# The same steps of a two-block layer stack on one core, merged in another order

## The reference, cut to what matters

```python
# block one, per layer: one wide projection, sparse attention beside a gated delta rule
proj = rms_norm(x, norm_gain[layer]) @ w_in[layer]                 # 1024 x 9304
y_a = dsa_attention(q_a, k_a, v_a, q_i, k_i, w_i) * silu(z_a)      # 64 keys of each query's indexer
o_b = chunked_gated_delta_rule(q_b, k_b, v_b, beta, g)             # needs a triangular inverse per chunk
x = x + (gate0 * y_a + gate1 * rms_norm(o_b) * silu(z_b)) @ w_out[layer]
...
x = rms_norm(x, final_gain)
# block two, per layer: projection, four attention branches, gated merge, output, layer norm
h = x @ w_in                                                       # 1024 x 3620
...
merged = merged + merge_g[:, :, n] * (yb @ w_branch[n])            # n = 0..3
out = merged @ w_out
x = layer_norm(ALPHA * x + out, ln_g, ln_b)
```

## Time and profile before

| | us |
|---|---|
| median of 3 runs | 1119.81 |
| lowest and highest | 1117.81, 1120.29 |
| the profiled execution, its own time | 1118.74 |
| its span in the trace | 1116.9 |
| PE busy | 1056.6 (95%) |
| POOL, DVE, ACT busy | 662.7, 624.0, 595.4 |

### The profile page before, as it was taken

One profiled execution on the slowest core, in us unless ns is written; L12 is line 12 of the kernel. 1 busy time (PEld: TensorE's weight loads), 2 busy tenths in 40 slices (PEclk: granted clock), 3 DMA queues, 4 the chain that ended last, 5 costly groups with the idle time before them and its releaser, 6 DMA issues.

```text
span 1116.9 us, 16760 instructions
## 1 busy us (share of the span) xinstructions
PE 1056.6 (95%) x6282; PEld 914.2 (82%) x6282; DVE 624.0 (56%) x1195; ACT 595.4 (53%) x998; POOL 662.7 (59%) x286
## 2 busy tenths in 40 slices
PE   5999999999979999999999998899999889999986
PEld 5988898888867897899888887788888668888865
DVE  3765349674555449526875555508455660645664
ACT  4654348654633574435665555345586534548651
POOL 3775446753626877445666445687545876754483
PEclk9999999999989999999999999899999999999999
DMA  8554235542333655342554333665333555533251
GB/s 293 167 173 130 82 113 151 151 133 76 113 132 111 186 170 151 97 131 82 152 145 132 95 114 106 179 187 153 100 103 96 191 162 170 151 118 105 87 190 53
DMA packets 80575, 151.59 MB, mean 136 GB/s; under 512 B 6448, under 2 KB 12400, under 8 KB 80496
## 3 DMA queue, kind: packets, MB, share of 16 engines
q1 hardware_dynamic: 80496, 150.54, 44.8%
HBM read 149.47 MB, written 1.05 MB: 135 GB/s over the span
## 4 chain that ended last, share of the span: by engine, by line
PE 85%; DVE 7%; ACT 3%; issue 2%; POOL 1%; DMA 1%; DVEq 0%; SPq 0%; ACTq 0%; POOLq 0%
PE bulk L905 49%; PE bulk L893 12%; PE chain L995 9%; PE chain L926 6%; PE bulk L898 1%; PE chain L1260 1%; PE chain L1241 1%; POOL w_lo L842 1%; PE chain L1115 1%; PE chain L1131 1%; DVE arena L1708 1%; ACT arena L1300 1%; PE chain L986 1%; DVE arena L1786 1%; DVE arena L1783 1%
## 5 line engine op out<-in xcount | busy, mean ns | idle before, releaser
L842 POOL TENSOR_TENSOR w_lo<-raw,w_hi 128x1024 fp32r<-128x1024 f32 (+4 forms) x277 | 648.8, 2357 | 431.7 <-ACT w_hi L1300 431.4
L1300 ACT ACTIVATE w_hi<-raw 128x1024 fp32r<-128x1024 f32 (+4 forms) x277 | 279.7, 1019 | 202.0 <-PE bulk L905 164.2
L905 PE MATMUL bulk<-w_hi,hT_hi 128*128 128x512 f32 (+1 forms) x756 | 308.5, 408 | 12.8 <-DVE arena L1786 6.6
L905 PE MATMUL bulk<-w_hi,hT_lo 128*128 128x512 f32 (+1 forms) x756 | 296.3, 392 | 0.0
L905 PE MATMUL bulk<-w_lo,hT_hi 128*128 128x512 f32 (+1 forms) x756 | 296.0, 392 | 0.0
L905 PEld LDWEIGHTS bulk<-w_hi,hT_hi 128*128 128x128 f32 x756 | 143.7, 190 | 47.9 <-DVE arena L1786 8.8
L905 PEld LDWEIGHTS bulk<-w_hi,hT_lo 128*128 128x128 f32 x756 | 143.4, 190 | 30.5
L905 PEld LDWEIGHTS bulk<-w_lo,hT_hi 128*128 128x128 f32 x756 | 143.9, 190 | 26.6 <-issue 1.0
L1300 ACT ACTIVATE arena<-chain 128x512 f32<-128x512 f32 (+4 forms) x92 | 62.0, 685 | 120.1 <-PE chain L926 106.2
L995 PE MATMUL chain<-arena 128*128 128x128 f32 (+1 forms) x864 | 113.7, 279 | 1.5 <-DVE arena L1964 0.7
L926 PE MATMUL chain<-cst,arena 128*128 128x128 f32 (+2 forms) x672 | 94.8, 279 | 20.2 <-DVE arena L1722 11.2
(11 more groups left out here) (249 smaller groups left out, 1288.3 us busy)
## 6 DMA issues: line engine op xcount, KB each, us to landing
raw<-in_w_in_dram SPq DMA_DIRECT2D x194, 512.0 KB, 3.6
raw<-in_w_out_dram SPq DMA_DIRECT2D x32, 512.0 KB, 4.3
raw<-in_w_branch_dram SPq DMA_DIRECT2D x16, 512.0 KB, 3.8
raw<-in_w_mem_kv_dram SPq DMA_DIRECT2D x8, 512.0 KB, 3.6
raw<-in_w_merge_up_dram SPq DMA_DIRECT2D x16, 256.0 KB, 2.8
raw<-in_w_in_dram SPq DMA_DIRECT2D x8, 420.0 KB, 3.3
gain<-in_ln_rows_dram SPq DMA_DIRECT2D x4, 512.0 KB, 5.5
gain<-in_gains_dram SPq DMA_DIRECT2D x3, 512.0 KB, 7.1
```

Source lines behind the costliest of these rows:

```text
L842: pool.tensor_tensor(lo_of(p, u)[:, 0:n], raw_of(p, u)[:, 0:n], hi_of(p, u)[:, 0:n].bitcast(F32), ALU.subtract).then_inc(p.done("split"), 1)
L905: m = pe.matmul(dst, a, b[:, k, :], start=(first and k == 0 and i == 0), stop=(last and k == nk - 1 and i == 2))
L1300: return act.activation(dst, src, func, **more)
```

## The change

Only the string `ORDER` is another one. Both strings hold 1186 letters, and each lane has as many letters as before, so the same steps run with the same operations, tiles and waits. The units are loaded in the same sequence and lie in the same slots. The merging differs nearly everywhere. Two lines of the string, which by themselves say nothing to a reader:

```diff
-    "aaaaasammssvaasasmmsaaaaascmmmccsssamcascccamsasammmcssasacmmmsmcasaascmasasmaamsaamdbmsmbsaamdmscma"
+    "aaaaasamsvsmamssmaassmaaaaasccsssmmccamaccmsmcaasamcssmasacsmmsmcmcasasamsaamdbssaamsmbaamcmmaasmmaa"
...
```

## The result

The changed kernel takes **1137.07 us** (median of 4 runs, 1135.96 to 1137.99) against 1119.77 us before: a ratio of 1.0157, 95% interval 1.014 to 1.0175. That is 17.3 us slower, where 3.0 were forecast and 1128 was the upper end of the range. Its profiled execution took 1135.96 us, with a span of 1133.9.

A forecast was written before the change was run, and what follows sets the result against it. The prediction took PE's work plus PE's waits as the bound. Its terms, 0.1 + 1.35 - 1.0 + 0.5 + 1.1 + 0.3 + 0.7 = +3.0 us, added to the median 1119.81, gave 1122.8 us, range 1117 to 1128.

The forecast's parts named there:

- A: Norm between the blocks: DVE's sums run freely, PE stops 3.8 us for POOL's later split; +0.1 us.
- B: Layer norm between block two's layers: one more DVE drain ahead of PE's first product; +1.35 us (0 to 1.4).
- C: ckT(1): a bulk product now stands ahead and covers PE's 1.04 us wait for DVE; -1.0 us.
- R1: Rival, chance 0.15: sums of squares between the blocks stay slow and PE stops 7.2 us; 1126.2 us.
- D: End of layer 0, block one: values product waits less, DVE's mixing comes later; +0.5 us (-0.9 to +1.4).
- E: The inverse: more small PE steps directly behind the one whose drain they need; +1.1 us (0 to 1.6).
- F: The start: the first tap moves behind one more split on ACT; +0.3 us (0 to 1.5).
- G: Attention in block two: three places lose the bulk product between two small steps; +0.7 us (0 to 1.5).
- R2: Rival, chance 0.14: DVE gets ahead of POOL at the layer norm, PE's 2.7 us wait goes; 1116.6 us.

The follow-up runs named there:

- f5: The changed kernel with POOL's subtraction of unit 76 of layer 0 made to wait for DVE's mix(1): 1131.91 us.
- e4: The changed kernel with DVE's gmul of g11 in layer 0 moved back to right behind memT(0): 1135.15 us.
- f3: The kernel before with POOL's first subtraction of block two's second layer made to wait for DVE's ln(0) of the first layer: 1119.82 us.
- f6: The kernel before with POOL filling the low half with zeros in 52 pieces a unit instead of subtracting: 1121.05 us.

## Why the prediction was wrong

The direction was right (slower had 0.52), but by luck: the three terms that rest on rows, A to C, came to -0.3 us together, and 12.7 of the 17 us lie in two places of layer 0, of which the sum had one at +0.5 and the other not at all. The size was missed by 14 us. The prediction's own sign of being wrong, another stop of over 2 us, came twice.

- **A, +0.1 forecast, +0.1 measured.** Its working held row by row. The sums run freely, the stop of PE is 3.5 us, and the second h1 product starts 15.33 us later than before (741.72 against 726.39), where a product of the output projection ahead of the norm started 15.25 later (702.33 against 687.08):

```profile
721.30 1.23 DVE L1708 CUSTOM_DVE_ANT_0 arena<-xs 128x1024 f32<-128x1024 f32 x1 [0.17 <-DVE xs L1745]
...
722.45 1.22 DVE L1708 CUSTOM_DVE_ANT_0 arena<-xs 128x1024 f32<-128x1024 f32 x1
...
728.73 0.50 PE L905 MATMUL bulk<-w_hi,sT_hi 128*128 128x512 f32 x1 [3.49 <-POOL w_lo L842]
```

  With it R1 falls. Read by its printed input, line 1708 should not have been held; the rows and these say that it was.
- **B, +1.35.** The wait of the product grew from 1.15 to 2.11 and the first product came 1.4 us later, as forecast; 0.5 was given back at once: +0.9.
- **C, -1.0.** PE no longer waits at `ckT(1)` and gained 1.3 us there.
- **D, +0.5 (-0.9 to +1.4).** This is the step that failed: +7.1. The wait at line 1131 shrank from 1.5 to 1.2 only, not to 0.6, and the mixing came 2.1 us later, 0.7 above the top of the range. Both are small. What the term left out is that I costed DVE's two instructions behind the mixing by their own time. The term had to ask, as A did, where POOL's subtractions would lie. In the earlier trace rows the neighbour of this stretch, eight instructions in 4.28 us, was itself held by 2 us (2.19 in f5), and I used it as a price without asking why it was so long. And DVE's lead over POOL before was 0.03 us at line 2171, so there was no bound of +1.4: the holding cost 2.0 us where one of the two lines lost (e4) and 3.9 where both did, and the half clock came behind it.
- **rep(1), not in the sum: +5.6.** "Everything else in the string exchanges steps whose partners are far apart, covered by at least one product of 2.7 us" was the second failure. `rep(1)` has such cover, but before, line 1908 ended 0.8 us ahead of PE's need, after a stretch in which DVE had 2.1 us of gaps. A step of 1.98 us more and some 5 us more of holding (9 us on this stretch of DVE, against 4 before, counting each row above its fastest time) used both up and made the stop.
- **E, F, G, +2.1 together.** Layer 1 has +3.4 and attention in block two +1.9; the start none. That is two and a half times what was said, and mostly by other means. In layer 1, 1.1 us are waits; 1.7 come from the stop of 3.99 us that was put down as untouched: it is, but the stretch at half clock behind it is 6.7 us long and not 3.3 as in the earlier trace rows (granted clock 0.72 from 690 to 702 us). In attention, PE waits 1.1 us at line 1209 and 0.9 more at line 905, each time for a DVE instruction that a subtraction held (line 2293, 2.19 us for 0.17; line 1786, 2.12 for 1.23).
- **R2** was the right mechanism at the wrong place: 0.3 us decided, at `mT(1)`, and for the slower side. I had priced the holding in two places that looked bad before, and not in those that were only just good. One reading was off as well: line 2360 in the earlier trace rows starts after POOL's row at 909.20 has ended, and was held by the next subtraction, from 911.56. So a lead of 0.24 us over the first would not have been enough, and f3 shows the later ones holding DVE.

## What to carry to other kernels

Where two engines shut each other out, an order that looks covered may hang on a few hundredths of a microsecond: look in the trace of before for instructions on the critical path that are fast only because the other engine started later, and price each at its held time. Take the duration of an instruction from its fastest row, and read every longer row as a meeting with someone. Moving one step away from a meeting mostly finds the next one; a wait that keeps the other engine out of the short chain that PE stands for may gain, but only where what comes behind it has slack.

## What the runs showed of the hardware

POOL's subtraction costs DVE 96 us of 624, about 15%, and with its length some 12 us of the whole kernel's time even in the better order (1106.6 with the short fill against 1118 to 1120). The size of the held instruction doesn't matter: one on a single column (line 1638) took 2.17 us for 0.16. A train of 52 small POOL instructions is worse for a `TENSOR_SCALAR` (5.67 us) than one long instruction (2.0 to 2.2 us more in the rows above). The custom sum of squares, printed with one input, behaves like an instruction with two: 3.28 us for 1.23 beside a subtraction, 1.23 beside the fills of f6. In the changed kernel a stop of PE of 3.7 us and one of 5.5 us both cost 1.6 to 1.8 us more in the half clock behind them, 3.4 us long each. That isn't a fixed price: behind the same stop of 3.7 us, f5 ran at half clock for 6.8 us (granted clock 0.62 from 231 to 240 us).
